# Expert rows by indexed transfers, the next rows turned a step sooner, and filler products on TensorE, in a two-layer encoder trunk in float32

## The reference

```python
logits = (t @ w_router)                       # t: 256 x 1024, 8 experts
top_vals, top_idx = lax.top_k(logits, 2)
gates = jax.nn.softmax(top_vals, axis=-1)
combine = jnp.sum(jax.nn.one_hot(top_idx, 8) * gates[..., None], axis=1)
for e in range(8):                            # expert width 3584
    y = y + combine[:, e:e + 1] * ((silu(t @ w1[e]) * (t @ w3[e])) @ w2[e])
```

## Time and profile before

| | us |
|---|---|
| median of three runs | 1520.61 |
| profiled execution / its span | 1523.13 / 1521.3 |
| up to the first expert product | 512.5 |
| expert part (7 runs of 125.15, the last and its end) | 1008.8 |
| TensorE busy / VectorE / ScalarE / GpSimd | 1451.0 / 1148.2 / 954.7 / 42.7 |
| moved by DMA | 424.67 MB, mean 279 GB/s |

### The profile page before, as it was taken

How to read it: one execution, slowest core, us unless ns; L and a number is a source line. 1 busy time by engine, 2 the same in 40 slices (tenths; PEclk the granted TensorE clock), 3 DMA queues, 4 the chain that set the end, 5 groups by cost and what they waited for, 6 DMA issues and landing times.

```text
span 1521.3 us, 20025 instructions
## 1 busy us (share of the span) xinstructions
PE 1451.0 (95%) x7249; PEld 1217.4 (80%) x7249; DVE 1148.2 (75%) x1049; ACT 954.7 (63%) x918; POOL 42.7 (3%) x79
## 2 busy tenths in 40 slices
PE   5788999998987899999999999999999999999998
PEld 5577999997876688878878878888887887887886
DVE  4665544546674889879888888888987998888894
ACT  4455433444563677767777777687776767677772
POOL 3120000000100000000000000000000000000000
PEclk9889999998999899999999999999999999999999
DMA  8145455554532599989989999998998998999992
GB/s 303 57 122 167 138 181 181 192 188 140 185 123 86 195 337 376 372 305 375 383 320 353 375 332 331 390 360 306 379 378 326 342 382 328 339 384 332 336 376 89
DMA packets 150625, 424.67 MB, mean 279 GB/s; under 512 B 11149, under 2 KB 41018, under 8 KB 150586
## 3 DMA queue, kind: packets, MB, share of 16 engines
q1 hardware_dynamic: 146752, 420.39, 76.0%
q10 hardware_dynamic: 3450, 3.69, 0.8%
q0 software_dynamic: 384, 0.07, 0.1%
HBM read 423.08 MB, written 4.19 MB: 281 GB/s over the span
## 4 chain that ended last, share of the span: by engine, by line
PE 93%; DVE 4%; ACT 1%; issue 1%; POOL 0%; DMA 0%; ACTq 0%; POOLq 0%; SPq 0%; DVEq 0%
PE ps L1370 82%; PE ps L1365 4%; PE ps L1693 2%; PE ps L1667 2%; PE ps L1484 2%; PE ps L1504 1%; DVE wl_a L919 1%; ACT wh_a L596 0%; DMA xr<-in_x 0%; ACT tn L605 0%; DVE kT L1047 0%; DVE bias L1062 0%; DVE xr L955 0%; PE ps L1645 0%; DVE htl L938 0%
## 5 line engine op out<-in xcount | busy, mean ns | idle before, releaser
L919 DVE TENSOR_TENSOR wl_a<-raw,wh_a 128x2048 fp32r<-128x2048 f32 (+1 forms) x230 | 516.0, 2270 | 123.1 <-ACT wh_a L596 123.1
L596 ACT ACTIVATE wh_a<-raw 128x2048 fp32r<-128x2048 f32 (+1 forms) x230 | 434.1, 1906 | 209.6 <-PE ps L1370 200.3
L919 DVE TENSOR_TENSOR wl_b<-raw,wh_b 128x2048 fp32r<-128x2048 f32 x168 | 378.8, 2286 | 35.4 <-ACT wh_b L596 34.3
L596 ACT ACTIVATE wh_b<-raw 128x2048 fp32r<-128x2048 f32 x168 | 319.3, 1925 | 56.5 <-PE ps L1370 53.3
L1370 PE MATMUL ps<-wh_a,hth 128*128 128x512 f32 (+2 forms) x576 | 226.3, 393 | 5.6 <-DVE htl L938 3.5
L1370 PE MATMUL ps<-wl_a,hth 128*128 128x512 f32 (+2 forms) x576 | 223.4, 388 | 0.0
L1370 PE MATMUL ps<-wh_a,htl 128*128 128x512 f32 (+2 forms) x576 | 223.4, 388 | 0.0
L1370 PE MATMUL ps<-wh_b,hth 128*128 128x512 f32 x448 | 178.4, 398 | 0.0
L1370 PE MATMUL ps<-wh_b,htl 128*128 128x512 f32 x448 | 174.6, 390 | 0.0
L1370 PE MATMUL ps<-wl_b,hth 128*128 128x512 f32 x448 | 174.4, 389 | 0.0
L1370 PEld LDWEIGHTS ps<-wh_a,hth 128*128 128x128 f32 x576 | 109.3, 190 | 30.1 <-issue 6.7
(11 more groups left out here) (230 smaller groups left out, 2050.9 us busy)
## 6 DMA issues: line engine op xcount, KB each, us to landing
raw<-in_moe_w SPq DMA_DIRECT2D x336, 1024.0 KB, 7.3
raw<-in_ffn_w SPq DMA_DIRECT2D x33, 1024.0 KB, 5.3
raw<-in_a_w_o SPq DMA_DIRECT2D x4, 1024.0 KB, 5.7
raw<-in_b_w_q SPq DMA_DIRECT2D x4, 1024.0 KB, 5.1
raw<-in_kv_w_k SPq DMA_DIRECT2D x4, 1024.0 KB, 5.1
raw<-in_kv_w_v SPq DMA_DIRECT2D x4, 1024.0 KB, 5.0
raw<-in_b_w_o SPq DMA_DIRECT2D x4, 1024.0 KB, 5.2
bias<-bias_wide ACTq DMA_DIRECT2D x8, 384.0 KB, 3.2
```

What stands on the lines that cost most here:

```text
L596: nc.scalar.activation(dst[:, 0:w], raw[:, n % RAW, 0:w], ACT.Copy).then_inc(hi_done, 1)
L919: nc.vector.tensor_tensor(l[:, 0:w], raw[:, n % RAW, 0:w], h[:, 0:w].bitcast(fp32), ALU.subtract).then_inc(lo_done, 1)
```

## The change

1. *Rows by indexed transfers.* GpSimd builds a table of which row stands in which slot of which run. Before layer 1 it zeroes `y_rows` in HBM and a few padding rows; after the last normalisation it writes `tn` to HBM, computes the addresses, scatters the row numbers into a table in HBM and reads the table back. In each run VectorE copies the run's column of it to `cur_s` and `cur_g` (`current`, in step 1), and GpSimd issues two indexed transfers: `ye`, the result of the run before, into `y_rows`, and the next run's rows from `tn_rows` into `tn[:, 0]`. The loop on GpSimd always has 11 turns; in the last run VectorE lets it do the three that are left (`spare`), with row numbers that nobody reads, and ScalarE waits for them before the last `ye`.
2. *One combine instead of nine.* All experts' results but the last are read back from `y_rows` at the end by two loads of 1 MB and added to `xr` with the gates as factors (`add_rows`). Only the last run still has `gpick` and `combine`.
3. *The next rows sooner.* Instead of `gather` before the last two units, PE transposes the new rows (`turn_rows`, 8 transposes) between `gate` and `lin` of step 3, and `gathered` on ACT and DVE follows behind `lin` of step 3. The transposes of step 3's gated product stand one unit earlier, before the last `down` unit of step 2, and `gt_hi` and `gt_lo` of step 3 with them.
4. *Filler products.* `keep_busy(n, bank)` puts n products of 256 columns in float32 that nobody reads into PE's list, where it waits: 26 before the first attention pair of layer 0, 8, 7 and 12 before the turns n1, n2 and n3, 6 and 2 in the routing, and single ones at the ends of both attentions.
5. `line_pad` grows by 64 bytes. The eight new small tiles take 704 bytes if each is rounded up to 32, so that the tiles behind move by 768, six times 128.

```diff
+BUSY = {"heads": 26, "n1": 8, "n2": 7, "n3": 12, "route": 6}
 # GpSimd
             norm(1)
+            chain(nc.gpsimd.memset(zeros, 0.0))
+            for r in range(2):
+                pool.dma_start(y_all[r, 0:SEQ, :].rearrange("(t p) d -> p t d", p=P), zeros).then_inc(y_put, 16)
...
             norm(3)
+            for t in range(T):
+                pool.wait_ge(tn_done, T * 3 + t + 1)
+                pool.dma_start(tn_rows[t * P:(t + 1) * P, :], tn[:, t, :]).then_inc(x_got, 16)
+            pool.wait_ge(tab_done, 1)
...
+            for r in range(2):
+                for t in range(T):
+                    nc.gpsimd.indirect_dma_start(slot_tab, bass.IndirectOffsetOnAxis(ap=addr[:, r, t:t + 1], axis=0),
+                                                 sent[:, r, t:t + 1], None).then_inc(sent_done, 16)
...
+            with pool.Fori(0, NE + V_EXTRA) as v:
+                pool.wait_ge(m_cur, v * 2 + 2)
+                pool.wait_ge(p_turn, v + 1)
+                pool.wait_ge(y_put, v * 16 + Y_INIT)
+                pool.wait_ge(x_got, v * 16 + X_INIT)
+                nc.gpsimd.tensor_tensor(step_, rev, rev, ALU.add).then_inc(p_turn, 1)
+                nc.gpsimd.indirect_dma_start(y_rows, bass.IndirectOffsetOnAxis(ap=cur_s[:], axis=0), ye[:], None).then_inc(y_put, 16)
+                nc.gpsimd.indirect_dma_start(tn[:, 0, :], None, tn_rows, bass.IndirectOffsetOnAxis(ap=cur_g[:], axis=0)).then_inc(x_got, 16)
 # ScalarE, run(v, final)
                     for i in range(e_units(c) + (e_units(c - 1) if c else 0)):
+                        if c == ESTEPS - 1 and i == e_units(c) and not final:
+                            act.wait_ge(unit_used, v * U_RUN + (U_MOE + e_first("lin", c) + e_units(c)))
+                            gathered(v + 1)
+                        if c == ESTEPS - 1 and i == e_units(c) + e_units(c - 1) - 1:
+                            gt_hi(v, c)
                         mhi(k + 4)
                         k += 1
-                gt_hi(v, ESTEPS - 1)
 # VectorE, run(v, final)
+                    if final and c == ESTEPS - 1:
+                        spare()
...
-                    else:
-                        add_run(v)
...
                     if c == 1:
-                        one_hots(v)
+                        current(v)
...
                     for i in range(e_units(c - 1) if c else 0):
+                        if c == ESTEPS - 1 and i == 1 and not final:
+                            gathered(v + 1)
+                        if c == ESTEPS - 1 and i == e_units(c - 1) - 1:
+                            gt_lo(v, c)
                         mlo(k + 4)
                         k += 1
-                gt_lo(v, ESTEPS - 1)
 # VectorE, after the loop
+            add_rows()
+            add_run()
 # TensorE
+            def keep_busy(n, bank):
+                for _ in range(n):
+                    mm(ps[bank][:, 0:256], ident, cst[:, 0:256], start=True, stop=True)
...
                     eup("gate", 0, c)
-                    if c == 0:
-                        combine(v)
-                    else:
+                    if c:
                         eturn(c - 1)
+                    if c == ESTEPS - 1 and not final:
+                        pe.wait_ge(x_got, v * 16 + (X_INIT + 16))
+                        turn_rows(v)
                     eup("lin", 2, c)
                     if c:
-                        edown(c - 1)
+                        edown(c - 1, range(e_units(c - 1) - (c == ESTEPS - 1)))
                 eturn(ESTEPS - 1)
...
-                if not final:
-                    halves = gather()
-                    next(halves)
-                    pe.wait_ge(m_gl, v * ESTEPS + ESTEPS)
-                    next(halves)
+                edown(ESTEPS - 2, range(e_units(ESTEPS - 2) - 1, e_units(ESTEPS - 2)))
                 edown(ESTEPS - 1)
```

More of the change, by code:

```diff
@@ L575, in _ @@
             norm(3)
+            for t in range(T):
+                pool.wait_ge(tn_done, T * 3 + t + 1)
+                pool.dma_start(tn_rows[t * P:(t + 1) * P, :], tn[:, t, :]).then_inc(x_got, 16)
+            pool.wait_ge(tab_done, 1)
+            posm, rank = work[:, 5], over[:, 1]
+            at, far, step_ = (place[:, i] for i in range(3))
+            both = place[:, 3:5]
+            nc.gpsimd.tensor_scalar(far, posm, float(P), None, ALU.is_ge)
+            chain(nc.gpsimd.tensor_tensor(step_, rev, rank.unsqueeze(1).to_broadcast([P, T, NE]), ALU.add))
@@ new lines, in _ @@
+            chain(nc.gpsimd.tensor_scalar(step_, step_, -float(P * SLOT_COLS), None, ALU.add))
+            nc.gpsimd.tensor_tensor(far, far, step_, ALU.mult)
+            chain(nc.gpsimd.tensor_scalar(at, posm, float(SLOT_COLS), float(NE + 1), ALU.mult, ALU.add))
+            chain(nc.gpsimd.tensor_tensor(at, at, rev, ALU.subtract))
+            chain(nc.gpsimd.tensor_tensor(at, at, far, ALU.add))
+            for r in range(2):
+                chain(nc.gpsimd.tensor_tensor(both[:, r], work[:, r], at, ALU.mult))
@@ new lines, in spare, with add_rows @@
+            def spare():
+                dve.wait_ge(y_put, runs * 16 + Y_INIT)
+                dve.wait_ge(x_got, runs * 16 + X_INIT)
+                chain(V.tensor_copy(cur_s[:], slots[:, 0:1]))
+                V.tensor_copy(cur_g[:], toks[:, 0:1]).then_inc(m_cur, 2 * V_EXTRA)
+            def add_rows():
+                for r in range(2):
+                    n = U_MOE + r
+                    dve.wait_ge(raw_here[n % RAW], 16 * (n // RAW + 1) + runs * (16 * U_RUN // RAW))
+                    for t in range(T):
+                        if r:
+                            dve.wait_ge(y_add, t + 1)
+                        V.scalar_tensor_tensor(xr[:, t, :], raw[:, n % RAW, t * D:(t + 1) * D], (g1_, g2_)[r][:, t:t + 1], xr[:, t, :],
+                                               ALU.mult, ALU.add).then_inc(y_add, 1)
+                dve.wait_ge(y_add, 2 * T)
@@ L1356, in _ @@
             run(last_run, True)
-            add_run(runs)
+            add_rows()
+            add_run()
         @block.tensor
@@ L1709, in eup, with edown @@
                         last.then_inc(unit_used, 1)
[L1711 to L1714 removed]
+                def edown(c, units=None):
+                    units = range(e_units(c)) if units is None else units
+                    if units[0] == 0:
+                        pe.wait_ge(m_gl, v * ESTEPS + (c + 1))
+                    if c == 0:
+                        pe.wait_ge(m_ye, v + 1)
+                    for h in units:
                         k = e_first("down", c) + h
```

153 lines of the change are left out of this document (104 added, 49 removed).

## The result

The changed kernel takes 1500.86 us, the median of four runs (1500.02 to 1501.72), against 1521.69 us (1520.49 to 1523.8) of the kernel before: 0.9862 of its time, with an interval of 0.9849 to 0.9876. It is faster by 1.4%. The forecast was 1476 us in a range of 1456 to 1497: the sign was right, but of the 44.6 us forecast less than half came, and the time lies above the range. The profiled execution took 1500.02 us; forecast for it were 1478.5. The question is where 21.5 us went.

What follows compares the result with a forecast made beforehand. TensorE was taken as the bound, with VectorE and the DMA close behind. The terms 50.7 - 16.1 - 2 + 12 gave 44.6 us saved, so the median of 1520.6 us became 1476, range 1456 to 1497.

Steps and rivals of the forecast that it cites:

- TensorE's list: In the expert part, combines, gathers and transposes leave TensorE's work: together 50.7 us gained.
- rival B: At each run's end no wait for `gtl`: a run of 118.6 us, 1460 us in all; chance 16%.
- the new wait: At the end of seven runs TensorE waits 2.3 us for `gtl`, none in the last: -16.1 us.
- the fillers' term: Ahead of the expert part, filler products keep TensorE's clock up: 12 us gained, of 17 at most.
- PEclk near 1.00 from 80 to 508 us: Sign that the forecast is right: TensorE's clock stays near full ahead of the loop.
- Rival C: Ahead of the expert part the fillers don't hold the clock, idle rests remain: 1488 us; chance 15%.
- the preparation on GpSimd: Around the loop's start, the table and GpSimd operations that hold VectorE up cost 2 us (0 to 8).
- the spare turns: In the last run, 38 us of TensorE's units cover three turns of 8 to 17 us: 0 us late taken.
- Rival D: In the last run, GpSimd's three spare turns wait for the port and delay the last `ye`: 1534 us; chance 7%.
- The criteria: The forecast is wrong if the loop's run is above 123 us or the first expert product comes after 506.

Runs made afterwards that it cites:

- Experiment 1: The changed kernel with VectorE doing `gt_lo` of step 3 ahead of `lo` 42 and `gathered` behind it: 1474.67 us.
- experiment 4: The changed kernel with five filler products put before the wait for `gtl` in all runs but the last: 1490.73 us.
- experiment 2: The changed kernel with 8 turns of GpSimd's loop instead of 11, so without spare turns: 1493.8 us.
- experiment 3: The changed kernel without any filler products: 1504.03 us.
- experiment 5: The changed kernel with GpSimd's zeroing and the slot table's start moved ahead of `norm(1)`: 1496.61 us.
- experiment 7: The changed kernel with VectorE's `lo` of expert unit 3 behind the first `gathered` instead of ahead of it: 1500.28 us.
- experiment 8: The changed kernel with 29 instead of 26 fillers before the first attention pair and two more before its first scores: 1498.54 us.
- experiment 6: The kernel before the change with the filler products alone added: 1516.2 us.
- the ninth kernel: The changed kernel with the edits of Experiment 1 and experiments 2, 5, 7 and 8 together: 1464.28 us.

## Why the prediction was half right

**Right: TensorE's list.** 50.7 us of combines, gathers and transposes leave the path. The run that was forecast at 120.9 us is 120.89. Experiment 1 shows the same without the wait, 118.31 against the 118.6 of rival B.

**Right: the new wait, in place, number and length.** Seven of 2.3 us, for `gtl`, none in the last run. Experiment 1 shows too that the wait came from the order of two VectorE groups and cost nothing to be rid of. `gtl` had 2.24 us of `lo` and 2.15 of `gathered` ahead of it that no product of the next 2.7 us needed. Rival B needed another order than this one.

**Wrong: what the wait costs.** The step was "TensorE waits 2.3 us, in each of seven runs: -16.1". The idle time was priced, the clock behind it was not. The same prediction had read from the earlier trace rows that the clock is half behind waits of 0.99 to 13.06 us, and it took the gain of the fillers from that; it did not carry this over to the wait that it added itself. With the 3.4 us at the half clock of the trace after, that is 1.7 us a wait, 12 in seven runs at most; measured were 8.2 in the profiled execution and 8.4 by experiment 4. The Trainium skill (TensorE: Matmul & The Clock Gate, section "HAM oscillation — how this bites in real kernels") says that waits which come back between groups of products can take the clock down each time. The trace agrees for five of seven waits; the two others show that such a wait needn't do it. Over the six profiled executions that have this wait (the changed kernel and experiments 2, 3, 5, 7 and 8) it was so behind 33 of 42, from four to six of seven in each. What decides it is open.

**Wrong: the fillers' term.** The step was "3.3, 2.5, 4.4 and 6.9, 17 in all ... so I take 3.5 and 3: 12 us". In the kernel before alone they are worth 6.7 (experiment 6), on the changed one 3.2. The stretches were priced as if a filled wait kept the clock for all that follows. But between the filled waits short ones stay, with 6.8 us at the half clock behind them at 154 and 492. And one ground for the price was misread: "each stretch before such a wait had the full clock" doesn't hold for the routing, where the earlier trace rows have 0.50 from 488 to 508, with both waits (500.94 and 504.24) inside. There the fillers ran in that half clock and took 4.51 us, not 2.7, longer than the wait that they were to fill. The sign "PEclk near 1.00 from 80 to 508 us" failed with this, by three stretches of 6.8 us. Rival C had this cause ("idle rests remain") but put the whole term at 0; by the experiments the term lies between its 0 and the forecast's 12.

**Wrong: the preparation on GpSimd.** It was priced at 2 us, with the table in mind. The table was hidden. What cost was the zeroing, placed where VectorE is on the path: 1.5 us of `tn` and the clock behind it, by experiment 5 4.3 us in the medians and 1.8 at the first expert product. Experiment 6 has all of the change but the fillers at 4.3 (504.37 against 508.71), with 3.6 to 6.2 between executions. So the zeroing is a part of it, and shown; what the rest is stays open. The half clock at 82 us, which experiment 6's execution doesn't have, may be some of it.

**Wrong: the spare turns.** The step was "`spare` stands where TensorE's list has unit 28, so 14 units or 38 us lie over its three turns". That is a miscount: the `lo` behind `spare` is unit 36's, so TensorE has unit 32 there, and ten units or 27 us lie over the turns. The trace has it so:

```profile
1453.65 0.39 PE L1494 MATMUL ps<-wh_a,hth 128*128 128x512 f32 x1
...
1455.80 0.14 DVE L1417 COPY cur_s<-slots 128x1 int32<-128x1 int32 x1
```

The first row is the start of unit 32, the second `spare`. A turn was 14.2, 7.6 and 7.3, one within the bounds of 8 to 17 and two just below; together they were 29.1 us, where 26 were left. So TensorE waited 3 us longer and then worked at half the clock: 5.2 by the rows, 7.1 by experiment 2. With ten units, the prediction's own bounds give 0 to 24 us late instead of 0 to 13. Rival D named the mechanism, and had it cost "from 12.7 us a turn on"; the mean of 9.7 cost something because 26 us lay over them, not 38. The kernel didn't come near to slower by it.

**The criteria.** The loop's run was to be under 123 and is (120.9 and 122.5). The first expert product was to come no later than 506 and is at 508.7: by this criterion the forecast was wrong, and it pointed to the right part, ahead of the loop.

With experiments 1, 2 and 5 the three wrong steps but the fillers can be mended in the kernel: 26.2, 7.1 and 4.3 us, 37.6 by their sum; the ninth kernel, with two small edits more, has 36.6.

## What to carry to other kernels

Price an idle stretch of TensorE with the clock behind it: look in the trace of before at what a wait of that length was followed by, and add it to each wait that a change brings in. Before a forecast stands, ask of each added wait which group ahead of the awaited one could stand behind it; here another order of two groups was worth more than the whole change had brought (26.2 against 20.8 us). Count in the list which unit stands beside a step before pricing what hides it. Put a filler only where the clock is full, since at the half it takes longer than the wait and is work on the path. And give work on an engine with time to spare a place of its own, since it costs by whom it stands beside.

## What the runs showed of the hardware

- An idle stretch of 2.3 us of TensorE, after a run of products without a pause, was followed by 3.4 us at half the clock in five cases of seven, and in 33 of 42 over six executions. With the same wait filled it never was (experiment 4). The stretch at 82 us had the half clock in the changed kernel's execution and the full one in experiments 6 and 7, with the same products there.
- A GpSimd memset, which reads nothing, of 1.81 us stretched a VectorE operation with one large input from 0.75 to 2.27 us; so it did in every profiled execution in which it stood beside it, and with the memset elsewhere (experiments 5 and 9) it is 0.75. The Trainium skill (SBUF — State Buffer, section "SBUF: two separate sides") lets the pair of ports be held by one instruction of either engine, and for VectorE's operations with one input this depends on the mode that they run in. The trace fits that: `tn` goes through 1024 floats in 0.75 us, `lo` through 2048 in 2.28, so `tn` is in a faster one. That the pair of ports is the cause is inferred, since no run here shows the ports.
- The issue of an indexed transfer of 128 rows occupies GpSimd for very different times: the gather took 15.2 to 17.4 us in the eight runs and 0.97 us in each of the three spare turns:

```profile
680.24 15.20 POOL L663 DMA_INDIRECT tn<-tn_rows,cur_g  x1 [0.30 <-issue]
...
1461.83 0.97 POOL L663 DMA_INDIRECT tn<-tn_rows,cur_g  x1 [0.30 <-issue]
```

  The loads don't explain it: the DMA moved 398 GB/s while the first of these was issued and 410 while the second was, and the scatters into `y_rows` were issued in 0.97 to 1.09 us in the middle of the runs. What sets the time is open.

- One core's DMA engines moved 381 GB/s through runs of 118.3 us, at a share of 0.99, and TensorE did not wait (experiment 1). The Trainium skill (DMA: Bandwidth & Descriptors, section "Where 436 GB/s comes from") has HBM's limit for a core at about 358 GB/s, a stack's bandwidth divided by two cores. The kernel here runs on one core; the measurement decides, and it is above that.
